# Loads, lists and rows asked for ahead of the stages that use them, a third fixed expert, and shorter routing picks

## The reference

```python
h = modulate(rmsnorm(x, g_mix), sh_a, sc_a)
q_sb, k_sb, v_sb, q_lat, kv_lat, kpe_raw = split(h @ w_in)
# eight stick-breaking heads of 64 and eight latent-attention heads (64 + 32), run side by side
x = x + gt_a * (concat(o_sb, o_mla) @ w_out)
h2 = modulate(rmsnorm(x, g_ffn), sh_m, sc_m)
group = argmax(h2 @ w_rg + b_rg)                    # one of 4 groups
top2 = top_k(h2 @ w_re + b_re inside the group, 2)  # two of its 8 experts
x = x + gt_m * sum(weight * (silu(h2 @ w_gate[e]) * (h2 @ w_up[e])) @ w_down[e])
```

## Time and profile before

| | |
|---|---|
| median of three runs | 1403.44 us (1402.46 to 1403.66) |
| the profiled execution | 1402.2 us, its span 1400.5 us |
| PE busy | 1239.2 us, 88% of the span |
| DVE, ACT, POOL busy | 708.3, 377.3, 211.8 us |
| HBM | 186.60 MB read, 35.71 MB written |
| mean granted clock of PE | 0.94 of full |

### The profile page before, as it was taken

How to read it: one execution, slowest core, us unless ns; L and a number is a source line. 1 busy time by engine, 2 the same in 40 slices (tenths; PEclk the granted TensorE clock), 3 DMA queues, 4 the chain that set the end, 5 groups by cost and what they waited for, 6 DMA issues and landing times. The chain is left out here.

```text
span 1400.5 us, 18449 instructions
## 1 busy us (share of the span) xinstructions
PE 1239.2 (88%) x6682; PEld 710.6 (51%) x6683; DVE 708.3 (51%) x1378; ACT 377.3 (27%) x839; POOL 211.8 (15%) x247
## 2 busy tenths in 40 slices
PE   4999999999859968699999999899927999989885
PEld 1555555555426646465666666555523444444342
DVE  1244554444547764266766764566642444444433
ACT  1121222222214451265544453233320000000000
POOL 0000000000000010243333231011131222212222
PEclk9999999999979988699999999899958999999997
DMA  9711111111149842212001004442219999999962
GB/s 363 265 40 60 49 41 60 60 46 34 45 140 298 281 145 53 85 30 54 19 10 27 1 1 153 158 181 91 77 62 414 341 374 368 373 340 349 339 236 33
DMA packets 108713, 213.33 MB, mean 152 GB/s; under 512 B 22321, under 2 KB 72611, under 8 KB 95330
## 3 DMA queue, kind: packets, MB, share of 16 engines
q1 hardware_dynamic: 100482, 195.05, 38.7%
q0 software_dynamic: 8160, 17.34, 5.1%
HBM read 186.60 MB, written 35.71 MB: 159 GB/s over the span
## 5 line engine op out<-in xcount | busy, mean ns | idle before, releaser
L2065 PE MATMUL g_GU<-w_gu,g_xT 128*128 128x512 f32 (+1 forms) x432 | 163.7, 597 | 2.1 <-DVE g_xT L2271 1.4
L1684 PE MATMUL f_C<-first_region,oT 128*128 128x512 f32 x256 | 115.0, 602 | 0.0
L415 PE MATMUL U<-w_in_sb,b_hT 128*128 128x512 f32 x256 | 112.3, 592 | 0.0
L2065 PEld LDWEIGHTS g_GU<-w_gu,g_xT 128*128 128x128 f32 (+1 forms) x432 | 64.2, 172 | 81.0 <-issue 80.3
L1508 DVE TENSOR_TENSOR_SCAN e_stick<-e_stick 128x128 f32<-128x128 f32 (+7 forms) x64 | 86.6, 1374 | 11.0 <-POOL e_stick L1318 11.0
L2080 PE MATMUL g_Y<-w_down,g_hT 128*128 128x512 f32 (+1 forms) x216 | 87.8, 618 | 0.5 <-issue 0.5
L415 PE MATMUL b_UL<-w_in_sb,b_hT 128*128 128x384 f32 (+2 forms) x272 | 80.0, 453 | 3.9 <-DVE b_hT L629 3.9
L2275 DVE TENSOR_TENSOR g_sig<-g_GU,g_sig 128x256 f32<-128x256 f32 x26 | 11.0, 424 | 141.0 <-ACT g_sig L2243 140.9
L1684 PEld LDWEIGHTS f_C<-first_region,oT 128*128 128x128 f32 x256 | 48.0, 193 | 54.1 <-issue 53.9
L415 PEld LDWEIGHTS U<-w_in_sb,b_hT 128*128 128x128 f32 x256 | 47.5, 190 | 54.2 <-issue 54.0
L1374 PE MATMUL e_Z<-first_region,work 96*128 96x512 f32 (+3 forms) x192 | 74.4, 515 | 0.0
(11 more groups left out here) (382 smaller groups left out, 2192.9 us busy)
## 6 DMA issues: line engine op xcount, KB each, us to landing
w_gu<-w_gate SPq DMA_DIRECT2D x27, 1024.0 KB, 13.0
w_gu<-w_up SPq DMA_DIRECT2D x27, 1024.0 KB, 26.7
w_down<-w_down SPq DMA_DIRECT2D x27, 1024.0 KB, 25.5
key_region<-w_ada SPq DMA_DIRECT2D x16, 1024.0 KB, 5.6
w_in_sb<-w_in SPq DMA_DIRECT2D x3, 2048.0 KB, 17.3
first_region<-w_gate SPq DMA_DIRECT2D x5, 1024.0 KB, 10.9
first_region<-w_up SPq DMA_DIRECT2D x5, 1024.0 KB, 23.5
first_region<-w_down SPq DMA_DIRECT2D x5, 1024.0 KB, 21.2
```

What stands on the lines that cost most here:

```text
L415: end = nc.tensor.matmul(dst[0:T, 0:c1 - c0], lhsT=hT[:, k, 0:T], rhs=g.w_in[:, k, c0:c1], start=k == 0, stop=k == KD - 1)
L1684: end = nc.tensor.matmul(C[n % 2][:, c * 512:(c + 1) * 512], lhsT=g.oT[:, k, i * P:(i + 1) * P], rhs=wo[:, k, c * 512:(c + 1) * 512], star ...
L2065: end = nc.tensor.matmul(GU[h * n:h * n + n, :], lhsT=xT[:, k, h * n:h * n + n], rhs=wgu[s][:, :, k, :], start=k == 0, stop=k == KD - 1, t ...
```

## The change

In B, the first tile's pieces of hT each raise `ht_first`, and PE's first product waits piece by piece in place of for `ht_done`. The first two tiles of CD's keys and latents get buffers of their own (`g.early`) and are asked for at the end of B. CD waits for its queries only ahead of the first scores, clears A's and B's semaphores on POOL, and asks at its end for E's first tile of earlier values. In E, each tile of vprev has its own semaphore, and the second difference is made behind the second unit. In FR, `picked` uses max and max_index on rows widened to 8 group columns (four of them are filled with -1e30); POOL clears two row buffers; SP asks for the third expert's weights once all projections are through (its buffer lies where w_out was); POOL asks for the lists of experts 0 and 1 at the end. FIXED is 3, so expert 2 is fixed too, and 29 are sorted. In G, POOL gathers for blocks 0 and 1 at once.

```diff
-FIXED, SINGLE = 2, 20
+FIXED, SINGLE = 3, 20
@@ B
             tiles(sp, body)
+            for t in range(2):
+                rows = slice(t * P, (t + 1) * P)
+                sp.dma_start(g.cc[:, t], io["cache_mla_ckv"][rows, :]).then_inc(g.cc_in[t], 16)
+                sp.dma_start(g.kc[:, t], io["cache_sb_k"][rows, :]).then_inc(g.kc_in[t], 16)
             queries_out(PT)
...
+            def project(dst, c0, c1, T, sem, follow=False):
                 for k in range(KD):
+                    if follow:
+                        pe.wait_ge(ht_first, k + 1)
...
-                pe.wait_ge(ht_done, i + 1)
                 if not first:
+                    pe.wait_ge(ht_done, i)
...
+                    project(UL[:, 0, :], 3 * SBW, 3 * SBW + QR, T, None, first)
...
+                    if isinstance(i, int) and i == 0:
+                        end.then_inc(ht_first, 1)
@@ CD
-                sp.dma_start(cc[:, b], io["cache_mla_ckv"][rows, :]).then_inc(cc_in[b], 16)
-                if later(t, 1):
-
+                    sp.dma_start(cc[:, b], io["cache_mla_ckv"][rows, :]).then_inc(cc_in[b], 16)
                     sp.wait_ge(kn_done, t - 1)
...
-                sp.dma_start(kc[:, b], io["cache_sb_k"][rows, :]).then_inc(kc_in[b], 16)
+                    sp.dma_start(kc[:, b], io["cache_sb_k"][rows, :]).then_inc(kc_in[b], 16)
...
+            sp.dma_start(g.vprev_first[1:113], io["o_v_p"][0:112, :]).then_inc(g.prev_in, 16)
+            sp.dma_start(g.vprev_first[113:P], io["o_v_p"][112:P - 1, :]).then_inc(g.prev_in, 16)
...
             nc.gpsimd.memset(qbd[:], 0.0).then_inc(z0, 1)
+            nc.clear_and_free_semaphores(g.retired)
...
+                if not later(t):
+                    pe.wait_ge(q_in, 64)
                 scores(t, lambda j: kT4[:, b, j, :], lambda h: kTm[:, h, :], P)
...
-            pe.wait_ge(q_in, 64)
@@ E
-            pool.wait_ge(prev_in, 16 * (PT + 1))
             pool.wait_ge(zero, 1)
 
             def differences(t):
+                pool.wait_ge(prev_in[t], 16 if t else 32)
...
             differences(0)
-            differences(1)
             for n in range(NU):
                 t, p = UNITS[n]
                 left(n)
                 scale(n)
+                if n == 1:
+                    differences(1)
                 if p == 0 and t + 2 < PT:
                     differences(t + 2)
@@ FR
+            sp.wait_ge(pr_mm, NT)
+            load_gate_up(nc, io, g, sp, 2, 2, g.wgu_in[2])
+            load_down(nc, io, g, sp, 2, 2, g.wd_in[2])
             sp.wait_ge(st_h2, 16 * NT)
...
+            for xg in g.xg:
+                nc.gpsimd.memset(xg[:], 0.0)
             pool.wait_ge(z_out, 16)
...
             for b in range(2):
                 pool.wait_ge(listed[b], 32 * len(range(b, NT, 2)))
+            for e in range(2):
+                nc.gpsimd.dma_start(g.li[e][:], g.list_dram[e * REGION:e * REGION + P, :]).then_inc(g.li_in[e], 16)
...
-                step(V.tensor_reduce(top[0:T, b, 0:1], lg[0:T, 0:NG], AX.X, ALU.max))
-                step(V.tensor_scalar(top[0:T, b, 1:2], top[0:T, b, 0:1], -1.0, None, ALU.mult))
-                first_max(og[0:T], lg[0:T, 0:NG], top[0:T, b, 0:1], T, NG)
+                step(V.max(gtop[0:T], lg[0:T, 0:GW]))
+                step(V.max_index(gat[0:T], gtop[0:T], lg[0:T, 0:GW]))
+                step(V.tensor_tensor(og[0:T], idx[0:T, 0:NG], gat[0:T, 0:1].broadcast_to([T, NG]), ALU.is_equal))
...
-                step(V.tensor_reduce(top[0:T, b, 2:3], masked[0:T], AX.X, ALU.max))
-                step(V.tensor_scalar(top[0:T, b, 3:4], top[0:T, b, 2:3], -1.0, None, ALU.mult))
-                first_max(pick[0:T, b, 0, :], masked[0:T], top[0:T, b, 2:3], T, NE)
-                step(V.scalar_tensor_tensor(masked[0:T], pick[0:T, b, 0, :], 3.0 * NEG, masked[0:T],
-                                            ALU.mult, ALU.add))
-                V.tensor_reduce(top[0:T, b, 4:5], masked[0:T], AX.X, ALU.max).then_inc(diff, 1)
+                step(V.max(etop[0:T], masked[0:T]))
+                step(V.max_index(eat[0:T], etop[0:T], masked[0:T]))
+                step(V.tensor_scalar(top[0:T, b, 0:1], gtop[0:T, 0:1], -1.0, None, ALU.mult))
+                V.tensor_tensor(top[0:T, b, 1:2], etop[0:T, 1:2], etop[0:T, 0:1], ALU.subtract).then_inc(diff, 1)
                 dve.wait_ge(diff, n + 1)
-                first_max(pick[0:T, b, 1, :], masked[0:T], top[0:T, b, 4:5], T, NE)
+                step(V.tensor_tensor(pick[0:T, b], idx[0:T].unsqueeze(1).broadcast_to([T, 2, NE]),
+                                     eat[0:T, 0:2].unsqueeze(2).broadcast_to([T, 2, NE]), ALU.is_equal))
@@ G
-            for b in range(FIXED):
-                list_in(b)
+            list_in(2)
...
-                else:
-                    pool.wait_ge(cleared, b + 1)
+                elif b >= 2:
+                    pool.wait_ge(cleared, b - 1)
                 gather(b % ROWSETS, li[b], xg_in[b % ROWSETS])
...
-            for r in range(ROWSETS):
-                nc.gpsimd.memset(xg[:, r, :], 0.0).then_inc(cleared, 1)
             for s in range(NB + ROWSETS):
+                if 2 <= s < ROWSETS:
+                    nc.gpsimd.memset(xg[s][:], 0.0).then_inc(cleared, 1)
                 if s < NB:
                     rows_in(s)
```

More of the change, by code:

```diff
@@ L631, in hT_of @@
                                                    ALU.mult, ALU.add)
-                end.then_inc(ht_done, 1)
+                    if isinstance(i, int) and i == 0:
+                        end.then_inc(ht_first, 1)
+                if not (isinstance(i, int) and i == 0):
+                    end.then_inc(ht_done, 1)
             def back(i, part):
@@ L1601, in phase_fr @@
         block = stack.enter_context(nc.Block())
-        bias = g.rows[:, ROWS["b_rg"][0]:ROWS["b_re"][1]]
         def tile(n):
@@ L1877, in normed @@
                 V.tensor_tensor(h2[0:T], h2[0:T], rows[0:T, 2, side, :], ALU.add).then_inc(h2_done, 1)
-            def first_max(out, values, peak, T, w):
-                step(V.tensor_scalar(eq[0:T, 0:w], values, peak, None, ALU.is_equal))
-                step(V.tensor_tensor(eq[0:T, 0:w], eq[0:T, 0:w], rev[0:T, 0:w], ALU.mult))
-                step(V.tensor_reduce(top[0:T, 0, 5:6], eq[0:T, 0:w], AX.X, ALU.max))
-                step(V.tensor_scalar(out, eq[0:T, 0:w], top[0:T, 0, 5:6], None, ALU.is_equal))
             def picked(n):
@@ L2398, in program @@
                 phase_a(nc, io, g)
+                mixed = ExitStack()
+                g.early = mixed.enter_context(nc.sbuf_tensor("early", [P, 1536], F32, side="right"))
+                g.kc = g.early[:, 0:1024].rearrange("p (b n) -> p b n", b=2)
+                g.cc = g.early[:, 1024:1536].rearrange("p (b n) -> p b n", b=2)
+                g.kc_in, g.cc_in = ([nc.alloc_semaphore(f"c_{n}{b}") for b in range(2)]
+                                    for n in ("kc", "cc"))
                 phase_b(nc, io, g)
-            mixed = ExitStack()
             g.o_s = mixed.enter_context(nc.sbuf_tensor("o_s", [DEC, D], F32, side="right"))
@@ L2407, in program @@
             g.q_m = g.work[0:MK, 8 * P:24 * P].rearrange("p (b h t) -> p b h t", b=2, t=P)
+            g.vprev_first = g.work[:, 24 * P:24 * P + SBW]
+            g.retired = list(USED)
+            USED.clear()
             phase_cd(nc, io, g)
@@ L2432, in program @@
         g.w_down.append(g.first_region[:, 2 * KD * DE:2 * KD * DE + 2 * D].rearrange("p (k n) -> p k n", n=D))
-        for b in range(FIXED + 1, 6):
+        g.xg = [m.sb(f"g_xg{r}", [P, D]) for r in range(2)]
+        g.li = [m.sb(f"g_li{b}", [P, 2], U32) for b in range(2)]
+        g.li_in = m.sems("g_li_in0 g_li_in1")
+        phase_fr(nc, io, g)
+        mixed.close()
+        for b in range(FIXED, 6):
             weight_slot(b)
```

104 lines of the change are left out of this document (54 added, 50 removed).

## The result

The changed kernel takes **1382.67 us** (median of 4 runs, 1380.71 to 1385.54); the kernel before took 1402.95 us on the same chip (4 runs, 1399.09 to 1403.66). The ratio is 0.9866, 95% interval 0.9845 to 0.9886: faster by 19 us, 1.3%. The forecast was 1385 with a range of 1372 to 1392. The profiled execution took 1384.27 us, its span 1382.4; the sum had said 1383.9 for it. That is near enough to be believed too quickly: the experiments show that two of its terms were off in size, in opposite directions, and that the mechanism of the largest one, though its size was met, was one of two limits.

A forecast was written before the change was run, and what follows sets the result against it. The prediction took PE to bound most stages and transfers to bound G after its start. Its terms, 0.3 + 0 + 8.3 + 9.7 = 18.3 us, gave 1383.9 for the profiled execution and 1385 for the median, range 1372 to 1392.

The forecast's parts named there:

- B: Start of tile stage B: first product goes piece by piece until the latent weights' load is late; 0.3 us gained.
- CD: Start of the cached-key stage: first product earlier, but the first sum waits for w_ada; 0, between 0.9 gained and 1.5 lost.
- E: Start of attention: PE's 8.5 us stall goes whole, 0.2 charged for the moved difference; net 8.3 us.
- FR's picks: End of routing: the last two picks on the path need fewer VectorE instructions; 3.3 us gained.
- Lists and rows ahead: Start of G: two list loads cost 2.5 us, gather comes earlier and takes 5.5; PE starts G 7.5 us earlier.
- The third expert ahead: Expert stage G: 3.1 MB less to move, 8.5 us; transfers limit, so G's end comes 9.7 us earlier.
- the stalls on lists vanish: Rival in G: PE keeps its earlier start and loses all later waits for rows; 1371 us, chance 0.15.
- the head of G gives little: Rival at G's start: gather still 8.4 us, searches cost double, list loads 4 us; 1390 us, chance 0.15.
- the stall of E only moves: Rival in attention: POOL's wait for tile 2's values holds the next units; 1393.5 us, chance 0.04.
- a list doesn't fit: Rival at G's end: a list exceeds its slot and takes the serial pass, about 35 us; 1420 us, chance 0.02.

The follow-up runs named there:

- the four corners: Changed kernel with neither, lists and rows ahead alone, third expert ahead alone, or both; last list scatter to last scatter 352.19, 352.46, 350.41, 344.74 us.
- lists by SP: Against the changed kernel, SP asks for the lists of experts 0 and 1 at the head of G, not POOL in routing; 1385.99 us.
- gathers earlier: Against the changed kernel, SP asks for lists two blocks ahead and POOL issues each gather of rows one block earlier; 1384.26 us.
- one more pair: Changed kernel with w_ada's first megabyte first and 18 single blocks, 7 pairs for 20 and 6; 1600.30 us, or 1596.33 with lists and gathers further ahead.

## Why the prediction was right, and where it wasn't

**B**: 0.3 forecast, 0.09 by the row. The load is late next, as said; its landing was 33.9, not 33.7.

**CD**: 0 forecast between 0.9 gained and 1.5 lost; 0.3 lost against the kernel before, 0.5 against the run without it. The argument held in each piece: the sum waits for `w_ada`, PE idles 4.58 us ahead of it, the second product is slow. The sentence that let the Trainium skill, TensorE: Matmul & The Clock Gate, section HAM oscillation, speak against this part was on the right side: a wait for transfers between bursts made the next burst start cold, and the trace agrees with 3.36 us for 1.95. The price was at most 0.3 to 0.5 us, within the spread, not the 1 worked out from it.

**E**: the stall of 8.5 us went whole, and what was charged for the moved difference never showed as a wait. The term still was mis-sized: 7.03 us in the profiled execution in place of 8.3. The step that failed is "A clock that rises sooner here may add half a microsecond; it is not counted". It took for granted that work moved 8.5 us ahead would be done at the same speed. The clock rose at about 588 in place of 591, so PE spent 19.5 us at work at the lower level in place of 14.8 (4.9 ahead of the stall, 9.9 behind it), and half of the 4.7 between them is lost: the third unit starts 9.0 us sooner than before (575.84 for 584.87), the fifth 8.0, the sixth and all later ones 6.9. In executions where it rose at about 577, E gained 10.6. Nothing in one trace of before could tell these apart; the range should have carried 2 us to either side for it.

**FR's picks**: 3.3 forecast between 2.0 and 3.8; 3.94 by the table, 4.2 by undoing them. The new instructions cost no more than the old, less indeed:

```profile
1012.02 0.17 DVE L1912 MAX8 f_gtop<-f_lg 128x8 f32<-128x8 f32 x1
...
1012.23 0.09 DVE L1913 MATCH_VALUE_LOAD f_gat<-f_gtop,f_lg 128x8 f32 x1
...
1012.31 0.16 DVE L1913 FIND_INDEX8 f_gat<-f_gtop,f_lg 128x8 uint32<-128x8 f32 x1
```

The Trainium skill, Vector Engine (DVE) Microarchitecture Reference, section 3.9, had each search as a load of the values plus a search. The trace agrees: the load is a row of its own. But at 0.09 us it is worth so little that the term it led to, 2.9, was further off than the one from the rows.

**Lists and rows ahead**: the two list loads cost 2.3 us between last scatter and opening (2.5 forecast), the gather 4.5 (5.5). PE's start came 8.5 us sooner after FR's start, 3.94 of it the picks (7.5 forecast).

**The third expert ahead** is the largest term, and its mechanism was half of what the runs show. "After its start, G is bound by transfers rather than by PE" and "3.1 MB less to move: 7.8 us at 402 GB/s, 9.1 at 344" made 8.5 us. Much of it came: the picks and G made 9.7 in the sum and 11.4 in the trace, undoing the part costs 7.7, and the late stalls are as forecast (the first shrank from 4.66 to 2.02 us, the next two are 4.57 and 3.95, before 4.60 and 3.87). The weights are a limit, if not one on which PE waits in either kernel: at the last three pairs they land 0.2 to 1.0 us ahead of PE's product in the kernel before, 0.5 to 3.3 in the kernel after, and once the rows come earlier PE waits 12.1 us for them. But the four corners show 7.7 us only together with the gather ahead and 1.8 without, and with lists by SP the end is 5.7 us later although the weights are early; a limit on transfers alone gives neither. What the term left out is the chain of scatters, which runs without a gap from the first pair nearly to the end. I had read the DMA share near 1 as the one bound. It is also a state of full queues, and makes each scatter land late: 10 to 11 us for 128 rows beside weights and 6 at the end of the stage, 8 and 4.3 for 64 rows. In the chain that ended last the scatter was in sight as its last row, with nothing behind it. The prediction reads none of POOL's own waits, which name the landing of scatters 23 times in the kernel after. In the kernel before they stand there too, as often, behind scatters of a single list:

```profile
POOL y L2045 <- DMA y<-g_y,g_li: 81.8, 17, 8.1
```

and in the kernel after:

```profile
POOL y L2062 <- DMA y<-g_y,g_li: 122.8, 18, 8.8
```

The 81.8 us of before were free to read. That POOL is no bottleneck by its busy time, 15% of the span, says nothing: it waits.

**The rivals.** That the stalls on lists vanish (1371): they do vanish with gathers earlier, weights take their place, and nothing is earned. That the head of G gives little: PE started G sooner than forecast. That the stall of E only moves: no. That a list doesn't fit: it fitted, but its price was far too small, 35 us worked out from transfers, where the pass costs 223; a chance of 0.02 then weighs 4.4 us and not 0.7.

**Open** is what decides when the clock rises in E, and how the 7.7 us of the third expert divide between the bytes themselves and the chain of scatters, whose landings the bytes delay. The runs with one more pair, which shorten the chain and leave the bytes of the weights, are not clear of the spread.

## What to carry to other kernels

When the shares say that transfers are full, ask of each engine that issues them what it waits for between two issues: here POOL, 15% busy, ran a chain of read-modify-write scatters, each behind the landing of the last, and PE's stalls for rows stood in its shadow. Take one stall away by an experiment before you add it to a sum: a stall that goes and leaves the end where it was names a limit behind it, and there can be two: here weights and scatters ended within a few us of each other. Terms that share the DMA engines (a gather and the weights issued a microsecond before or behind it) don't add; find which of them is issued first.

## What the runs showed of the hardware

The granted clock stayed at 0.50 for 19 us of a PE that was busy 23.1 of 24 us (568 to 592, the kernel after), and in another run with the same code of E it rose 11 us earlier, which is 3.6 us of E. A scatter that adds 128 rows of 4 KB to memory landed after 9.8 to 11.6 us beside weight loads and after some 6.1 without them, one of 64 rows after 7.6 to 8.6 and some 4.3 (the run with gathers earlier). A gather of 128 rows of 4 KB took 4.5 us when issued 1.1 us ahead of 3 MB of weights and 9.4 when issued 0.4 behind their first load. The value load of a search is 0.09 us, the search 0.16 to 0.19, and a maximum of eight 0.17 to 0.20, at 128 x 8 to 128 x 32. One list of 66 for 64 places, with its loops of register loads, compares and branches on every engine, added 223 us (that the loops cost it, and not the single pass, is argued from POOL's idle time alone).
